# Stick breaking with queries on partitions: running sums on VectorE and transposed weights in place of triangular matmuls on TensorE

## The reference

```
z = einsum('bhtd,bhsd->bhts', qb, kb) * scale
strict = s_idx < t_idx
log_1m = where(strict, log_sigmoid(-z), 0.0)
suffix = cumsum(log_1m, axis=3, reverse=True) - log_1m
a = where(strict, exp(log_sigmoid(z) + suffix), 0.0)
outs.append(einsum('bhts,bhsd->bhtd', a, vb))
```

## Time and profile before

| | us |
|---|---|
| median of 3 runs | 1318.77 (1318.74 to 1320.74) |
| the profiled execution's own time | 1319.46 |
| its span | 1317.7 |
| TensorE busy | 1296.9 (98%) |
| VectorE busy | 854.7 (65%) |
| ScalarE busy | 707.7 (54%) |
| stick-breaking stage, first projection to last output product | about 445 to 575 |

### The profile page before, as it was taken

How to read it: one execution, slowest core, us unless ns; L and a number is a source line. 1 busy time by engine, 2 the same in 40 slices (tenths; PEclk the granted TensorE clock), 3 DMA queues, 4 the chain that set the end, 5 groups by cost and what they waited for, 6 DMA issues and landing times.

```text
span 1317.7 us, 17683 instructions
## 1 busy us (share of the span) xinstructions
PE 1296.9 (98%) x7329; PEld 1119.3 (85%) x7329; DVE 854.7 (65%) x995; ACT 707.7 (54%) x968; POOL 111.2 (8%) x177
## 2 busy tenths in 40 slices
PE   7999999999999999999999999999999999999999
PEld 6889897988888888889888888898877888788887
DVE  4556664776666744377576666668785566787775
ACT  4654544644444577865454444555556654645553
POOL 7200100100000100020100000101330003000000
PEclk9999999999999999999999999999999999899999
DMA  8753643555555444244255555553444445355552
GB/s 259 247 169 131 205 162 118 186 192 192 191 192 191 166 157 159 96 160 160 97 191 194 190 191 192 174 195 112 160 135 153 160 129 191 128 192 191 192 192 96
DMA packets 156113, 223.64 MB, mean 170 GB/s; under 512 B 6103, under 2 KB 107635, under 8 KB 156032
## 3 DMA queue, kind: packets, MB, share of 16 engines
q1 hardware_dynamic: 154240, 218.18, 49.4%
q0 software_dynamic: 1664, 4.27, 1.0%
q10 hardware_dynamic: 128, 0.05, 0.0%
HBM read 221.44 MB, written 1.05 MB: 169 GB/s over the span
## 4 chain that ended last, share of the span: by engine, by line
PE 92%; DVE 3%; ACT 2%; POOL 1%; issue 1%; DMA 1%; SPq 0%; POOLq 0%; ACTq 0%
PE ps L397 19%; PE ps L421 9%; PE ps L399 9%; PE ps L423 9%; PE ps L422 9%; PE ps L382 5%; PE ps L383 5%; PE ps L384 5%; PE ps L559 4%; PE ps L561 4%; PE ps L560 4%; DVE wlo L1564 1%; PE ps L853 1%; PE ps L446 1%; ACT whi L1062 1%; PE ps L494 1%
## 5 line engine op out<-in xcount | busy, mean ns | idle before, releaser
L1062 ACT ACTIVATE whi<-raw 128x1024 fp32r<-128x1024 f32 x412 | 426.1, 1053 | 356.2 <-PE ps L397 167.5
L1564 DVE TENSOR_TENSOR wlo<-raw,whi 128x1024 fp32r<-128x1024 f32 x411 | 494.0, 1231 | 188.0 <-ACT whi L1062 184.6
L397 PE MATMUL ps<-RR,whi 128*128 128x512 f32 x1056 | 366.3, 398 | 0.8 <-DVE RR L1594 0.8
L399 PE MATMUL ps<-RR,wlo 128*128 128x256 f32 x1056 | 274.2, 280 | 0.1
L421 PE MATMUL ps<-whi,RR 128*128 128x512 f32 x592 | 237.6, 401 | 3.7 <-DVE ar L1627 1.6
L423 PE MATMUL ps<-whi,RR 128*128 128x512 f32 x592 | 231.3, 391 | 0.0
L422 PE MATMUL ps<-wlo,RR 128*128 128x512 f32 x592 | 231.1, 390 | 0.0
L397 PEld LDWEIGHTS ps<-RR,whi 128*128 128x128 f32 x1056 | 191.8, 189 | 37.6 <-DVE wlo L1564 1.2
L399 PEld LDWEIGHTS ps<-RR,wlo 128*128 128x128 f32 x1056 | 200.2, 190 | 12.3 <-DVE RR L1594 0.4
L382 PE MATMUL ps<-RR,whi 128*128 128x256 f32 x512 | 147.3, 288 | 1.7 <-DVE RR L1594 1.3
L383 PE MATMUL ps<-RR,whi 128*128 128x256 f32 x512 | 145.5, 284 | 0.0
(11 more groups left out here) (333 smaller groups left out, 1267.5 us busy)
## 6 DMA issues: line engine op xcount, KB each, us to landing
raw<-in_ffn_w_gate_up SPq DMA_DIRECT2D x44, 1024.0 KB, 5.0
raw<-in_ffn_w_down SPq DMA_DIRECT2D x33, 1024.0 KB, 4.8
raw<-in_w_in SPq DMA_DIRECT2D x28, 1024.0 KB, 4.9
raw<-in_ffn_w_up SPq DMA_DIRECT2D x22, 1024.0 KB, 5.0
raw<-in_xa_w_kv SPq DMA_DIRECT2D x16, 1024.0 KB, 5.1
raw<-in_sb_w_qkv SPq DMA_DIRECT2D x12, 1024.0 KB, 5.1
raw<-in_ml_w_in SPq DMA_DIRECT2D x11, 1024.0 KB, 5.7
raw<-in_xa_w_q SPq DMA_DIRECT2D x8, 1024.0 KB, 5.1
```

The source lines that it names most:

```text
L397: m = pe.matmul(two(ps[:, bank, :]), p.hi[:, k, :], XT2[:, k, :, :], start=k == 0, stop=k == 7)
L399: pe.matmul(ps[:, bank, 0:256], p.lo[:, k, :], X.h[:, k, :], start=False, stop=False)
L1062: act.activation(p.hi, p.raw, ACT.Copy).then_inc(S["w_hi"], 1)
L1564: dve.tensor_tensor(p.lo, p.raw, p.hi.bitcast(F32), ALU.subtract).then_inc(S["w_lo"], 2 if p.n == 2 else 1)
```

## The change

Queries now lie on partitions and keys along the free axis. In `sb_scores` the operands change places (query stationary, keys moving; the mask likewise). ScalarE's Abs, Exp, Ln are as before. VectorE's `sb_sums(p)` now makes softplus, runs one `tensor_tensor_scan` per head over 384 columns backwards (`within` is 1, and 0 at the two places where a new query block begins, which restarts the sum), and subtracts the result from the scores (all into `Sp`). ScalarE takes Exp of `Sp` in place (`sb_exps`). TensorE turns the weights by six transposes (`sb_turn`), into the banks of the scores, and VectorE copies them into `Aw` (`sb_turned`). `sb_scores(p)` now waits for that copy of pair p - 2 (semaphore `sb_c`). `sb_weights`, `triN` and `onesN` are gone. One activation table set that holds both Exp and Ln is loaded ahead of `squares(3)`. The loop over i is written out on all engines with pieces interleaved by hand, `sbk3` comes ahead of `sbv1` in the weight order, and the output products `sbo2` and `sbo3` are done by first pieces, then second pieces.

```diff
-        for name, c in (("sbq2", 512), ("sbk2", 1536), ("sbq3", 768)):
+        for name, c in (("sbq2", 512), ("sbk2", 1536), ("sbq3", 768), ("sbk3", 1792)):
             chunk(name, W[:, c:c + 256], "c")
         tm_block("sbv1", W, 2560)
-        chunk("sbk3", W[:, 1792:2048], "c")
...
+                if p >= 2:
+                    pe.wait_ge(S["sb_c"], p - 1)
...
-                    m = pe.matmul(o[:, 0:256], kT[r, p, 0:128], qT[r, p, :], start=False, stop=False, skip_group_check=True)
+                    m = pe.matmul(o[:, 128:384], qT[r, p, 128:256], kT[r, p, :], start=False, stop=False, skip_group_check=True)
...
-            def sb_weights(p):
-                pe.wait_ge(S["sb_sp"], p + 1)
+            def sb_turn(p):
+
+                pe.wait_ge(S["sb_a"], p + 1)
                 for h in range(2):
-                    o = ps[:, 4 + 2 * (p % 2) + h, :]
-                    s = Sp[p % 3][:, h, :]
-                    pe.matmul(o[:, 0:256], triN[:, :], s[:, 0:256], start=False, stop=False, skip_group_check=True)
-                    pe.matmul(o[:, 128:256], onesN[:, :], s[:, 256:384], start=False, stop=False, skip_group_check=True)
-                    m = pe.matmul(o[:, 256:384], triN[:, :], s[:, 256:384], start=False, stop=True, skip_group_check=True)
-                m.then_inc(S["sb_w"], 1)
+                    for j in range(3):
+                        c = slice(128 * j, 128 * j + 128)
+                        m = pe.transpose(ps[:, 4 + 2 * (p % 2) + h, c], Sp[p % 3][:, h, c], ident[:, :])
+                m.then_inc(S["sb_t"], 1)
...
+            keys(1, 3, 0, M)
+            sb_turn(5)
+            sb_values(4)
+            sb_scores(7)
+            pe.wait_ge(S["K_act"], 4)
+            tm_tile("sbo0", sb_O, 0, 8, 0, 0)
+            sb_turn(6)
+            tm_tile("sbo0", sb_O, 0, 8, 2, 1)
+            sb_values(5)
+            tm_tile("sbo1", sb_O, 0, 8, 1, 0)
+            sb_values(6)
+            pe.wait_ge(S["sb_lo"], 3)
             tm_tile("sbo1", sb_O, 0, 8, 3, 1)
...
+            act.preload_act_table_set("natural_log_exp_and_others")
             squares(3)
...
+            def sb_exps(p):
+                act.wait_ge(S["sb_w"], p + 1)
+                act.activation(Sp[p % 3], Sp[p % 3], ACT.Exp).then_inc(S["sb_a"], 1)
...
+            def sb_sums(p):
+
+                b, s = 4 + 2 * (p % 2), Sp[p % 3]
+                dve.wait_ge(S["sb_ln"], p + 1)
+                dve.wait_ge(S["dve_step"], step(dve.scalar_tensor_tensor(s, ps[:, b:b + 2, 0:384], 0.0, s, ALU.max, ALU.add)))
+                for h in range(2):
+                    z = step(dve.tensor_tensor_scan(s[:, h, ::-1], within, s[:, h, ::-1], 0.0, ALU.mult, ALU.add))
+                dve.wait_ge(S["dve_step"], z)
+                dve.tensor_tensor(s, ps[:, b:b + 2, 0:384], s, ALU.subtract).then_inc(S["sb_w"], 1)
+
+            def sb_turned(p):
+                b = 4 + 2 * (p % 2)
+                dve.wait_ge(S["sb_t"], p + 1)
+                dve.tensor_copy(Aw[p % 2], ps[:, b:b + 2, 0:384]).then_inc(S["sb_c"], 1)
...
+            past("sbv0a")
+            sb_sums(1)
+            sb_turned(0)
...
+            lo_to(end("K1_3") - 1 + NSP)
+            sb_sums(6)
+            past("K1_3")
+            sb_turned(5)
+            sb_turned(6)
+            sb_sums(7)
```

More of the change, by code:

```diff
@@ L409, in tm_tile @@
             def tm_tile(name, X, k0, K, bank, t):
[L411 to L423, removed]
+                for i in range(2):
+                    m = tm_piece(name, X, k0, K, bank, t, i)
                     if t:
@@ L736, in sb_values @@
                 m.then_inc(S["sb_v"], 1)
[L738 to L791, removed]
@@ new lines, in tensor_program @@
+            sb_turn(2)
+            sb_values(1)
+            fm_piece("sbq3", X, 2, 1)
+            sb_scores(4)
+            pe.wait_ge(S["sb_q"], 3)
+            fm("sbk3", X, 0)
+            sb_turn(3)
+            sb_values(2)
+            tm_tile("sbv1a", X, 0, 8, 1, 0)
+            sb_scores(5)
+            pe.wait_ge(S["sb_q"], 4)
+            tm_tile("sbv1a", X, 0, 8, 2, 1)
+            tm_tile("sbv1b", X, 4, 8, 1, 0)
+            sb_turn(4)
+            sb_values(3)
+            tm_tile("sbv1b", X, 4, 8, 2, 1)
@@ new lines, in scalar_program @@
+            hi_to(end("sbk2") - 1 + NSP)
+            sb_exps(2)
+            sb_logs(3)
+            past("sbk2")
+            hi_to(end("sbq3") - 1 + NSP)
+            sb_out(0)
+            sb_q(3)
+            sb_exps(3)
+            sb_logs(4)
+            past("sbk3")
+            sb_exps(4)
+            sb_logs(5)
+            past("sbv1a")
+            sb_out(1)
+            past("sbv1b")
+            evac(Vs[:, 1, 512:1024], "sbv1b", 2, "sbv_act")
+            sb_exps(5)
+            sb_logs(6)
@@ L1350, in scalar_program @@
+            past("K1_3")
+            act.wait_ge(S["w_used"], end("K1_3"))
+            act.activation(Kx[:, 6:8, :], two(ps[:, 0, :]), ACT.Copy).then_inc(S["K_act"], 1)
+            sb_exps(6)
+            sb_logs(7)
+            past("sbo0")
+            sb_out(2)
+            sb_exps(7)
+            past("sbo1")
+            hi_to(end("sbo2") - 1 + NSP)
+            sb_out(3)
             past("sbo2")
@@ new lines, in vector_program @@
+            sb_sums(0)
+            sb_k(1)
+            past("sbv0a")
+            sb_sums(1)
+            sb_turned(0)
+            first_tile(Vs[:, 0, 0:512], "sbv0b", 1, "sbv_dve")
+            past("sbv0b")
+            lo_to(end("sbq2") - 1 + NSP)
+            sb_sums(2)
+            past("sbq2")
+            sb_turned(1)
+            sb_k(2)
+            sb_sums(3)
+            lo_to(end("sbq3") - 1 + NSP)
+            sb_turned(2)
+            sb_rest(0)
+            past("sbq3")
+            lo_to(end("sbk3") - 1 + NSP)
@@ new lines, in vector_program @@
+            sb_sums(4)
+            sb_k(3)
+            sb_turned(3)
+            past("sbv1a")
+            sb_sums(5)
+            sb_turned(4)
+            first_tile(Vs[:, 0, 512:1024], "sbv1b", 1, "sbv_dve")
+            sb_rest(1)
+            past("sbv1b")
+            lo_to(end("K1_3") - 1 + NSP)
+            sb_sums(6)
+            past("K1_3")
+            sb_turned(5)
+            sb_turned(6)
+            sb_sums(7)
+            past("sbo0")
+            sb_rest(2)
+            sb_turned(7)
@@ L1849, in vector_program @@
+            past("sbo1")
+            lo_to(end("sbo2") - 1 + NSP)
+            sb_rest(3)
             past("sbo2")
```

217 lines of the change are left out of this document (114 added, 103 removed).

## The result

The changed kernel took 1323.2 us (median of 11 runs, 1321.0 to 1325.46), beside 1319.43 of the kernel before on the same chip (1318.61 to 1320.94): a ratio of 1.0026, 95% interval 1.0017 to 1.0034. It is slower by a quarter of a per cent. The profiled span is 1321.6 us. The page's first row answers to the earlier trace rows; TensorE is busy for 5.2 us less, VectorE for 26 us more, ScalarE for 20 us less, and the span is 3.9 us longer.

The account below looks back on a forecast made before the run. TensorE, busy 98% of the span, was taken as the bound. Its own work -11.2, waits +11.4, table load +1.3 and stage end +0.8 gave +2.3 us on the median of 1318.77: 1321.0 us, range 1311 to 1328.

Parts of the forecast that it names:

- The clock falls at pair 7's wait: Rival: behind the 3.9 us wait matmuls run at half pace for 4 to 6 us, costing 2 to 3; 1323.5, chance 0.25.
- The seven waits, +11.4: TensorE waits for VectorE's copy at the scores of pairs 2 to 7, and ahead of `sbo1`: +11.4 us together.
- VectorE's prices: In the stage: 0.95 us per 384-column scan, backwards and in place free; sums 3.8 us, copy about 0.95; 30 us in all.
- the rival of dear scans: Rival: backwards scans cost up to 1.8 us, sums grow by 1.7; 1333, or 1325 with a third of that; chance 0.10.
- The one of short waits: Rival: cheaper scans or overlapping steps leave the waits absent or half as long; 1315, or 1309.7 without any; chance 0.22.
- TensorE's own work, -11.2: In the stage: `sb_weights` gone (-15.6 us), the end's wait gone (-1.4), transposes added (+5.8); scores and values unchanged.
- the transposes and values stand close before the wait: Argument against the clock's fall at pair 7: TensorE is at work shortly before the 3.9 us wait.
- the waits of 1 to 2 us are too short for it: Argument against the clock's fall: the other waits at the scores, 1 to 2 us, are too short to lower it.
- The table load at the start, +1.3: One load ahead of `squares(3)` is not covered and delays the first projection by its full 1.28 us: +1.3 us.
- The end of the stage, +0.8: VectorE's last addition comes some 1.2 us later, so TensorE waits 0.7 us for the `wlo` of `V1_1b`: +0.8 with hand-over.
- ScalarE's loads, worth nothing: Seventeen table loads of 1.283 us leave the pairs, 21.8 us of ScalarE's time, worth nothing directly since they lie beside matmuls.

Follow-up runs that it names:

- the copies first: Changed kernel with VectorE's copy of pair p - 1 ahead of the sums of pair p, p from 1 to 6: 1311.6 us, ratio 0.9945 to the kernel before.
- The late scores: Changed kernel with pair 7's scores issued one output tile later, behind the first tile of `sbo0`: 1318.88 us, ratio 0.9997 to the kernel before.
- pair 5's copy: Changed kernel with only pair 5's copy of turned weights moved ahead of pair 6's sums on VectorE: 1318.18 us, ratio 0.9993 to the kernel before.
- the preload early: Changed kernel with the joint table set loaded ahead of `post_squares(2)` instead of `squares(3)`: 1322.63 us, ratio 1.0027 to the kernel before.
- all moves: Changed kernel with copies ahead of sums, the early preload, and `sb_rest(2)` ahead of `past("sbo0")`: 1310.86 us, ratio 0.994 to the kernel before.

## Why the prediction came out as it did

The forecast was 1321.0 and the time is 1323.2, inside the range and on its slower side. The rival *The clock falls at pair 7's wait* gave 1323.5 and is the one that happened in the profiled execution. It seems to have happened in most of the others: those with a mean clock of 0.997 and more took 1321.0 to 1322.2, those with 0.995 and 0.996 took 1323.0 to 1325.5. The mean alone doesn't name the place, since the clock also falls near 1130 us in the trace before (mean 0.997) and in this one; two such falls make the 0.995.

That the forecast lies so near is in part luck: misses of +5.2 and -3.5 us nearly cancel (last paragraph of this section). The account of why TensorE waits was right; the clock, TensorE's own work and the price of the table load were not.

- **The seven waits, +11.4.** Right in kind and place. By the rows of the change, forecast were 1.6, 1.0, 1.6, 1.75, 0.85 and 3.9 at the scores and 0.65 ahead of `sbo1`; the rows have 1.49, 0.77, 1.30, 1.48, 0.50, 3.83 and 0.27: 9.6 us. The mechanism, a copy that stands behind the sums in VectorE's order, is shown by the moves: with the copies ahead, 0.24 us of it are left.
- **VectorE's prices.** The scan of 384 columns took 945 ns against 0.95, the block of sums 3.78 against 3.8 (the terms given for it add up to 3.7), the copy 952 ns. Running backwards and in place added nothing to the 0.95 read off the other scans, so the rival of dear scans is out. The one of short waits is out too.
- **TensorE's own work, -11.2.** Too large a saving. The stage grew by 4.06 us. Take off the waits (10.1 with that of `V1_1b`, in place of 1.43) and the clock (2.9, below), and -7.5 is left where -9.8 was forecast (-15.6 + 5.8). Added up from the starts of the blocks in both traces, the triangles had taken 15.3 us and the transposes take 5.5; scores (1.18 a pair at full clock) and values are as before. What was put at nothing is that the same chunks, cut up by more small products, take longer: the nine `fm` chunks 52.9 us instead of 52.5, the 19 output and value tiles 54.5 instead of 52.4 (slow stretch taken off), 2.5 in all. The rows show it at the seams. A tile in a row with others takes 2.73 us, one that stands alone between small products 2.76 to 3.03; the second matmul behind an interruption starts 0.22 us behind the first in an `fm` chunk, where 0.12 is the rule; and where TensorE stops, the last matmul is followed through the array before the wait begins to count (0.39 us for a tile's, where the next would have started after 0.23), so that each wait costs about 0.16 us more than its row. With the copies first, where most waits are gone, 1.8 of the 2.5 are left.
- **The clock.** The forecast kept it at 1.0 behind the 3.9 us at pair 7, on the argument that *the transposes and values stand close before the wait*. That step failed: they stood there, and the clock fell. In the profiled execution the scores of pair 7 took 2.1 us instead of 1.2, and `sbo0`'s first tile 4.85 (549.31 to 554.16) instead of 2.86 (two tiles in such a place, behind scores and ahead of transposes, take 5.59, 0.13 more than 2 x 2.73): 2.9 us. The late scores and pair 5's copy each took the fall away together with the wait. The other half of the argument, that *the waits of 1 to 2 us are too short for it*, held in this trace (1.49 us at pair 2, clock 1.00) but not in all the others (last section). The Trainium skill (TensorE: Matmul & The Clock Gate, "What's actually happening") has it that idle time halves the clock; the trace agrees at pair 7.
- **The table load at the start, +1.3.** This term was mis-sized: it is 0.3, alone in the kernel before as in the changed one. The squares came late by the whole load and a little more: 4.48 us behind VectorE's first row of the norm before (430.63 to 435.11), 5.91 now (430.31 to 436.22). What I missed is that GpSimd, next in the chain, was itself being held up before. Rows of the kernel before, then of the changed one:

```profile
435.81 2.36 DVE L1564 TENSOR_TENSOR wlo<-raw,whi 128x1024 fp32r<-128x1024 f32 x2
...
436.34 0.74 POOL L2147 TENSOR_SCALAR st<-st 128x1 f32<-128x1 f32 x1 [2.11 <-ACT xn L1080]
...
437.16 1.41 POOL L2148 TENSOR_TENSOR st<-st,mhalf 128x1 f32<-128x1 f32 x1
```

```profile
434.92 1.28 ACT L1319 ACT_TABLE_LOAD   x1
...
435.50 2.35 DVE L1603 TENSOR_TENSOR wlo<-raw,whi 128x1024 fp32r<-128x1024 f32 x2
...
436.22 1.06 ACT L1101 ACTIVATE xn<-xr 128x1024 f32<-128x1024 f32 x1
...
437.46 0.45 POOL L2217 TENSOR_SCALAR st<-st 128x1 f32<-128x1 f32 x1 [3.54 <-ACT xn L1101]
...
437.99 0.55 POOL L2218 TENSOR_TENSOR st<-st,mhalf 128x1 f32<-128x1 f32 x1
...
445.20 0.39 PE L384 MATMUL ps<-RR,whi 128*128 128x256 f32 x1 [0.51 <-DVE RR L1633]
```

  Before, GpSimd's two operations lie beside VectorE's two `wlo` pieces (435.81 to 438.17) and take 0.74 and 1.41 us: the first ends with the first piece, the second 0.4 us after the second. A load later, they meet the last 0.4 us of the pieces, take 0.45 and 0.55, and most of the delay is made good. The Trainium skill (GPSIMD Engine Reference, "Specifications") has a cause that fits: GpSimd shares its interfaces to SBUF with VectorE, with contention when VectorE's instruction has two inputs in SBUF, as `raw` and `whi` are. These rows agree with it. The long and the short durations follow the pieces in four traces (long before and with the preload early, short in the changed kernel and with the preload alone); a kernel with the pieces moved away wasn't run.
- **The end of the stage, +0.8.** The wait is 0.41, and the stretch from the last output matmul to `V1_1b`, whose two tiles between are the same, grew by 0.6. Right in kind, a little less in size.
- **ScalarE's loads, worth nothing.** Right for the kernel before: without them it took the same time. It would be wrong for the changed order, where without the preload the seventeen loads cost 9 us. The same instruction is free or dear by what stands behind it.

The misses, in the two traces: TensorE's own work +2.3, clock +2.9, the seven waits -1.7, the wait of `V1_1b` -0.4, the table load -1.0, and -0.4 outside the stage. Sum +1.7 us; the forecast change was +2.3 and the spans differ by 3.9. The medians differ by 3.8. The median missed by 2.2 because, besides, the kernel before had a median of 1319.43 beside the changed one and not the 1318.77 from which the forecast started.

## What to carry to other kernels

When steps move from TensorE to an engine with room, price the engine's queue, not its share: for each instruction that frees a buffer, add up what stands ahead of it since its own input was ready. A copy of 1 us behind sums of 4 us made the whole saving into a loss, and moving it ahead, with no instruction added or taken, gave 0.55% against the kernel before. A wait of some us on TensorE is to be counted with the slow stretch that may follow it, here 2.9 us behind 3.8.

## What was not expected of the hardware

- The clock fell behind each wait at the scores of 2.39 us and more: 3.83 (changed kernel, and two others), 4.23, 3.13, 3.12 and, with the scans left out, 2.39. It stayed at 1.00 behind 1.49, 1.30 and 1.48 us in the profiled execution of the changed kernel. Between them it went either way. Behind 1.53 us at pair 2 it fell with the preload earlier (0.50 at 486 to 488) and stayed at 1.00 with pair 5's copy first, where TensorE's order up to there is the same; behind 1.75 us it fell (0.62 at 544 to 546, without the preload). The waits near 1128 us, where the clock falls in the trace before, left it at 1.00 in the traces of the late scores and of all moves. So the length of the wait alone doesn't decide it. What else does stays open.
- Operations of GpSimd on 128x1 elements vary with what VectorE does beside them. Of the two shown above, the first takes 0.19 us at 430.68 in the kernel before, beside VectorE's `xn<-ps,grow`, which has one of its two inputs in PSUM, and 0.74 beside the pieces, which have both in SBUF. The second takes 0.55 us with VectorE idle and 1.41 beside the pieces. But the first takes 0.75 us also beside `xn<-xr,st` (at 438.66 before, 438.62 now), which has one large input, so pieces with two inputs in SBUF are not all that lengthens it.
